# Attention values and output projection by token tile, in matmuls of 512 columns

## The reference, cut to what matters

```python
h = rms_norm(x, norm_mix)
z = h @ w_in                        # queries, keys, values of branch A, gates ga, gb, ...
oa = moba_attention(qa, ka, va, bias_a) @ w_oa
ob = dsa_attention(qb, kb, vb, q_idx, k_idx, w_idx, bias_b) @ w_ob
x = x + (sigmoid(ga) * oa + sigmoid(gb) * ob) @ w_out
x = x + memory_cross_attention(rms_norm(x, norm_x), rms_norm(mem, mem_norm), wq, wk, wv, wo)
x = x + hier_moe(rms_norm(x, norm_moe), ...)   # 32 experts, 2 per token; w1, w3, w2: 6 MB each expert
return rms_norm(x, final_norm)
```

## Time and profile before

| | us |
|---|---|
| median of 3 runs | 676.24 |
| lowest, highest | 675.78, 677.32 |
| the profiled execution | 677.62 |
| its span | 675.8 |
| PE busy in it | 508.3 (75%) |
| DVE, ACT busy | 204.1 (30%), 145.3 (21%) |
| moved by transfers | 244.21 MB, mean 361 GB/s |
| mean granted PE clock | 0.88 |

### The profile page before, as it was taken

The page is one execution under the profiler, slowest core; times in us unless marked ns, Lnnn a source line. Parts: engine busy times, 40 slices in busy tenths (PEclk is TensorE's granted clock), DMA queues, the critical chain, the costliest instruction groups (busy, mean ns, idle before and its releaser), DMA issues.

```text
span 675.8 us, 8749 instructions
## 1 busy us (share of the span) xinstructions
PE 508.3 (75%) x3793; PEld 322.9 (48%) x3793; DVE 204.1 (30%) x376; ACT 145.3 (21%) x252; POOL 16.5 (2%) x31
## 2 busy tenths in 40 slices
PE   7999999999999997966834835773474567347475
PEld 6999998899999752421401411231131123114121
DVE  4799655488857431100000100000010000001002
ACT  5665555354535421000000000000000000000002
POOL 1200010001001000000000000000000000000001
PEclk8999999999999998996867978785798869679779
DMA  9899433607899999999999999999999999999994
GB/s 291 257 324 366 184 125 125 249 1 261 299 392 384 405 387 430 429 426 429 428 428 430 424 432 427 427 430 423 432 428 426 430 427 428 429 426 430 426 407 158
DMA packets 48825, 244.21 MB, mean 361 GB/s; under 512 B 9032, under 2 KB 18704, under 8 KB 37264
## 3 DMA queue, kind: packets, MB, share of 16 engines
q1 hardware_dynamic: 48784, 243.62, 89.3%
HBM read 242.53 MB, written 4.22 MB: 365 GB/s over the span
## 4 chain that ended last, share of the span: by engine, by line
PE 52%; DMA 43%; SPq 2%; issue 1%; ACT 0%; DVE 0%; PEld 0%; POOL 0%; POOLq 0%; PEldq 0%; DVEq 0%
PE ps L707 16%; DMA slots_late<-in_w 13%; PE ps L1065 11%; DMA slots_own<-in_w 9%; DMA attn_data<-in_w 7%; PE ps L730 7%; PE ps L1070 6%; DMA slot_last<-in_w 5%; DMA slot_mixed<-in_w 5%; DMA slot_spare<-in_w 3%; PE ps L685 1%; PE ps L758 1%; SPq L542 1%; PE ps L824 1%; PE ps L853 1%; PE ps L1174 1%
## 5 line engine op out<-in xcount | busy, mean ns | idle before, releaser
L1065 PE MATMUL ps<-slots_late,x_sb 128*32 128x512 f32 x320 | 85.4, 676 | 35.9 <-DMA slots_late<-in_w 14.1
L1065 PE MATMUL ps<-attn_data,x_sb 128*32 128x512 f32 x160 | 63.4, 700 | 12.4 <-DMA slots_own<-in_w 12.4
L1065 PE MATMUL ps<-slot_spare,x_sb 128*32 128x512 f32 x128 | 59.6, 664 | 15.9 <-DMA attn_data<-in_w 15.9
L1801 DVE TENSOR_TENSOR slot_extra<-ps,slot_extra 128x512 f32<-128x512 f32 x8 | 5.5, 692 | 213.0 <-ACT slot_extra L1428 213.0
L433 DVE TENSOR_TENSOR w_low<-slots_own,w_high 128x2048 fp32r<-128x2048 f32 (+1 forms) x32 | 64.6, 2021 | 15.9 <-ACT w_high L1238 15.7
L1425 ACT ACTIVATE slot_extra<-ps 128x256 f32<-128x256 f32 x8 | 3.1, 383 | 299.6 <-PE ps L1132 299.6
L1065 PE MATMUL ps<-slots_own,x_sb 128*32 128x512 f32 x240 | 55.5, 654 | 9.5 <-DMA slot_spare<-in_w 3.9
L1070 PE MATMUL ps<-slots_own,slot_extra 128*32 128x512 f32 x192 | 49.0, 715 | 17.1 <-DMA slots_late<-in_w 8.3
L1238 ACT ACTIVATE w_high<-slots_own 128x2048 fp32r<-128x2048 f32 (+1 forms) x32 | 54.2, 1696 | 18.4 <-PE ps L730 10.8
L1070 PE MATMUL ps<-attn_data,slot_extra 128*32 128x512 f32 x112 | 45.8, 747 | 15.1 <-DMA slots_own<-in_w 15.1
L707 PE MATMUL ps<-h_high,w_high 128*128 128x256 f32 x224 | 55.4, 288 | 0.0
(11 more groups left out here) (258 smaller groups left out, 869.5 us busy)
## 6 DMA issues: line engine op xcount, KB each, us to landing
slots_own<-in_w SPq DMA_DIRECT2D x27, 2048.0 KB, 32.7
slots_late<-in_w SPq DMA_DIRECT2D x25, 2048.0 KB, 35.0
attn_data<-in_w SPq DMA_DIRECT2D x16, 2048.0 KB, 34.2
slot_last<-in_w SPq DMA_DIRECT2D x9, 2048.0 KB, 34.9
slots_own<-in_w_in SPq DMA_DIRECT2D x8, 2048.0 KB, 12.1
slot_spare<-in_w SPq DMA_DIRECT2D x8, 2048.0 KB, 35.4
slot_mixed<-in_w SPq DMA_DIRECT2D x7, 2048.0 KB, 35.0
slots_own<-in_w_out SPq DMA_DIRECT2D x2, 2048.0 KB, 8.5
```

The costliest lines, as they stand in the source:

```text
L1065: return pe.matmul(ps[SLOTS * e:SLOTS * e + SLOTS, 4 + matrix, :], xeT[:, k, SLOTS * e:SLOTS * e + SLOTS], w, start=(k == 0), stop=(k == K ...
```

## The change

Two helpers are added. `half_depths` computes the first or second half of the depths of two jobs at once: of 512 weight columns, for both token tiles, in matmuls of 128 x 512. A job is now one token tile by 512 columns, and a unit of split weights is 4 depths by 512 columns (the same size as before). `keep_warm` issues matmuls of zeros. The rest follows from this: which bank comes free when, what the additions and turns wait for, and in what order ACT and DVE do their part. Beside this, units 8 and 9 of the expert weights come in halves, and one `start_sum` moves.

```diff
-EARLY_HALF = {10: 0, 11: 1}
+EARLY_HALF = {8: 0, 9: 0, 10: 0, 11: 1}
+FIRST_HALVES = ("av0", "out0", "out2")
 # weights()
+            if stem in ("av", "out"):
+                return c, w512(c)[:, 4 * (i % 2):4 * (i % 2) + 4, :]
 # sync, behind the load into place 3
                     weights_split(sp, "vm")
-                    load_half(10, EARLY_HALF[10], early_half_in[10])
+                    for early in (10, 8, 9):
+                        load_half(early, EARLY_HALF[early], early_half_in[early])
 # tensor
 gains_turned():
                 pe.transpose(ps[:, 1, 0:KD], gain_rows, ident[0:KD, 0:KD]).then_inc(gain0_turned, 1)
+                keep_warm(1)
 turn_residual(b):
-                pe.wait_ge(resid_set, b + 1)
+                pe.wait_ge(resid_set, b // 2 * 2 + 2)
+            def half_depths(tiles, second, ready=None):
+                unit = tiles[second]
+                wh, wl = part(w_high, unit), part(w_low, unit)
+                for low in range(2):
+                    if low:
+                        weights_split(pe, unit)
+                    else:
+                        pe.wait_ge(split_high, SPLITS.index(unit) + 1)
+                    for t in range(TT):
+                        if not second and not low:
+                            begin(tiles[t])
+                        o = ps[:, job(tiles[t])[0], :]
+                        for k in range(4):
+                            depth = 4 * second + k
+                            if ready and t + low == 0:
+                                ready(depth)
+                            for x_ in (h[:1] if low else h):
+                                m = pe.matmul(o, x_[:, depth, t * P:(t + 1) * P], (wl if low else wh)[:, k, :],
+                                              start=(depth + low == 0 and x_ is h[0]),
+                                              stop=(low == 1 and depth == KD - 1), skip_group_check=True)
+                        if second and low:
+                            end(m, tiles[t])
+                if not second:
+                    m.then_inc(wide_used, 1)
+            def keep_warm(n):
+                for _ in range(n):
+                    pe.matmul(ps[:, 6, 0:P], score[:, 0:P], score[:, 0:P], start=True, stop=True)
             pe.wait_ge(zeros_set, 1)
-            for _ in range(14):
-                pe.matmul(ps[:, 6, 0:P], score[:, 0:P], score[:, 0:P], start=True, stop=True)
+            keep_warm(16)
             turn(xn, xn_set, gains_turned)
+            keep_warm(2)
-            split_rows("av0", h)
+            half_depths(("av0", "av1"), 0)
             scores(0)
-            split_rows("av1", h)
+            half_depths(("av0", "av1"), 1)
-            for i in range(4):
-                split_rows(f"out{i}", h, merged_ready if i == 0 else None)
-                if i:
-                    turn_residual(i - 1)
+            for i in range(2):
+                half_depths(("out0", "out1"), i, merged_ready)
+            half_depths(("out2", "out3"), 0)
+            turn_residual(0)
+            turn_residual(1)
+            half_depths(("out2", "out3"), 1)
             query_products(0, q0, range(4))
+            turn_residual(2)
             turn_residual(3)
-            start_sum(1, 0)                # of the three ahead of the routing
+                    start_sum(1, 0)        # beside the fourth, in step 0
 # scalar: split_weights(u)
+                if u >= 2 and SPLITS[u - 2] in FIRST_HALVES:
+                    act.wait_ge(wide_used, FIRST_HALVES.index(SPLITS[u - 2]) + 1)
+                elif u >= 2:
 # scalar: values
-            for i in range(2):
-                copy_job(f"av{i}", av[:, :, 256 * i:256 * i + 256], by_rows)
-                after(f"av{i}")
-                if i == 0:
-                    exps(0)
+            after("av0")
+            exps(0)
+            for t in range(TT):
+                copy_job(f"av{t}", av[:, t, :])
+            after("av1")
 # scalar: output projection
+            after("out0")
+            after("out1")
+            split_turned(2, 0, 2, tT_high)
+            split_turned(2, 1, 2, tT_high)
+            after("out2")
+            act.wait_ge(resid_set, 3)
             square(x_sb[:, 0, :], 2, 0, xn[:, 0, :], squares[0])
+            split_turned(2, 2, 2, tT_high)
             split_turned(2, 3, 2, tT_high)
 # vector: output projection
+            after("out0")
+            for t in range(TT):
+                add_residual(f"out{t}", x_sb[:, t, 0:512], resid_set)
+            after("out1")
+            split_turned(2, 0, 2, tT_high, tT_low)
+            split_turned(2, 1, 2, tT_high, tT_low)
+            after("out2")
+            for t in range(TT):
+                add_residual(f"out{2 + t}", x_sb[:, t, 512:1024], resid_set)
+            split_turned(2, 2, 2, tT_high, tT_low)
             square(x_sb[:, 1, :], 2, xn[:, 1, :])
             split_turned(2, 3, 2, tT_high, tT_low)
```

More of the change, by code:

```diff
@@ L124 @@
           + [f"ob{i}" for i in range(4)] + ["km"] + [f"out{i}" for i in range(4)] + ["qx", "vm"])
+assert SPLITS.index("qx") % 2 == EARLY_HALF[8] and SPLITS[-1] == "vm"
+FIRST_HALVES = ("av0", "out0", "out2")
 STEP_JOBS = [("av0", "av1"), ("ga0", "ga1"), ("ga2", "ga3"), ("bq0", "bq1"), (None, "gb0"), ("gb1", "oa0"),
@@ L313, in decoder_layer @@
         h_high_set, h_low_set = sem("h_high_set"), sem("h_low_set")
-        split_high = sem("split_high")
+        split_high, wide_used = sem("split_high"), sem("wide_used")
         low_set = (sem("low_set_v"), sem("low_set_p"))
@@ L1234, in split_weights @@
                 weights_landed(act, name)
-                if u >= 2:
+                if u >= 2 and SPLITS[u - 2] in FIRST_HALVES:
+                    act.wait_ge(wide_used, FIRST_HALVES.index(SPLITS[u - 2]) + 1)
+                elif u >= 2:
                     job_computed(act, SPLITS[u - 2])
```

## The result

The changed kernel takes 679.75 us, median of 20 runs (675.13 to 683.47); the kernel before took 676.26 in the 20 runs beside it (674.58 to 680.16). The ratio is 1.0045 (95% interval 1.0029 to 1.006): slower, clear of noise, by 3.5 us between the medians and 3.0 by the ratio, where 673.7 was forecast. The changed kernel's runs lie 8.3 us apart; those of the kernel before lie 5.6 apart, and 3.0 without the one at 680.16.

A forecast was written before the change was run, and what follows sets the result against it. TensorE's chain was taken to bound the first 250 us, the weight stream the expert part; values 1.2 plus output projection 1.3 gave 2.5 us off the 676.24 median, so 673.7 us, 8-in-10 range 672.3 to 676.5.

The forecast's parts named there:

- The values' term: Attention values on TensorE: wide calls let gate job ga0 start at 68.5, not 69.74; 1.2 us taken, bounds 0 to 1.24.
- at SP's own pace: Bias transfer ahead of ga0: asked for independently of PE, landing at 63.9 whatever PE does.
- Warming: Zero matmuls near the first turns: keep the clock up, PE up to 2.4 us earlier at 21; booked 0.
- this gain ends at the place above: Start of ga0: warming's earlier PE is stopped by the bias, since ga0 can't start before 68.5.
- Rival E: Before the router: PE idles 0.86 us more, clock drops to 1.2 GHz before the first request; 677.6 us, chance 0.08.
- Width: Split projections: one 512-column fp32r matmul costs 0.2145 us against two of 256 at 0.240; a call 5.15 us.
- Output projection: Output projection through queries: four wide calls save 2.4 us, new 1.0 us wait ahead of qx0; 1.3 gain taken.
- Rival C: Wide matmuls bring little or twos cost more: output loses 0.45 to gains 0.5, values 0 to 1.2; 675.6, chance 0.20.
- The halves and the third start_sum: Half transfers of expert units 8 and 9 fill a dip; the moved sum lies where PE waits anyway; 0 booked.
- the request moves the end: First further expert weights, asked for at 246.34: bringing that forward brings the end forward by the same amount.
- Rival D: Weight stream not done when the request comes earlier: only its own 1.2 us comes through; 675.0 us, chance 0.07.
- Rival B: Front gains more: warming's 2 us pass 68.5 because the bias lands earlier too; 671.7 us, chance 0.10.

The follow-up runs named there:

- a_cold: Changed kernel without its added warming (14 zero matmuls at the start, none between or behind the turns): 681.53 us, ratio 1.0084.
- a_kept_warm: Changed kernel with 14 matmuls on the identity between the values and ga0: 678.89 us, ratio 1.0048.
- a_bias_late: Changed kernel with one added 1 MB transfer right ahead of the bias read: 683.97 us, ratio 1.011.
- a_copies_first: Changed kernel with ACT's copies of the values ahead of exps(0) and DVE's low split of ga0 ahead of logits(0): 675.13 us, ratio 0.9981.
- a_narrow_values: Changed kernel with the values in two narrow jobs again, av0 copied ahead of exps(0): 675.82 us, ratio 0.9993.
- b_wide_values: Kernel before with only the values in wide matmuls and both copies behind exps(0): 678.7 us, ratio 1.0036.
- probe: Changed kernel with six forms of matmul, eight each, between the two calls of the values, into an unread bank: 692.34 us, one run, time not compared.
- b_warm: Kernel before with only the added warming (16, 1 and 2 matmuls of zeros): 675.6 us, ratio 0.9993.
- b_again: Kernel before, unchanged, profiled once more: 674.39 us in that execution.
- a_bias_early: Changed kernel with SP asking for the three bias transfers earlier, ahead of other loads: 678.47 us, ratio 1.0032.

## Why the prediction was wrong

**The values' term: gain 1.24, bound 0 below. This step failed.** I wrote that the bias "lands at 63.9 whatever PE does" and let ga0 start at 68.5 from it. The mechanism behind that was right: ga0 starts behind ACT's copy of av0, behind exps(0), 4.50 us after the first scores (64.98 to 69.48, and the same in a_cold, a_kept_warm and a_bias_late), where I had 4.55. What was wrong is that the landing was taken for a constant, and that the wait for it was priced at nothing. In the changed kernel's profile the first scores came at 64.98, 1.03 later, so ga0 gained 0.26 at its start instead of 1.24; and the wait of 3.12 let the clock fall, with which ga0 took 7.52 instead of 5.76 (1.5 of it the clock, the rest the start after a wait). The term came out at a loss of 1.5. That the order of the copies is the cause is shown from both sides: a_copies_first and a_narrow_values take the loss away, b_wide_values makes most of it.

I also wrote that the bias is asked for "at SP's own pace". It is not: SP waits until the copy within DRAM has landed (35.87 + 17.79 in the changed kernel's chain), and asks then. SyncE's rows for the read of the bias in the kernel before, profiled again, in the changed kernel, and in a_copies_first:

```profile
52.74 0.37 SPq L504 DMA_DIRECT2D attn_data<-bias_rep_dram  x1
```
```profile
53.68 0.37 SPq L509 DMA_DIRECT2D attn_data<-bias_rep_dram  x1
```
```profile
55.80 0.37 SPq L509 DMA_DIRECT2D attn_data<-bias_rep_dram  x1
```

In the nine profiled executions that leave the bias path alone (the probe aside), the first scores came at 63.70, 63.95, 64.21, 64.54, 64.98, 65.30, 66.96, 67.05 and 67.73, each after a wait. The copy was asked for at 35.2 to 37.3 and took 16.4 to 18.6 us, the read behind it 11 to 13. The old order takes such landings in its slack (a_narrow_values and b_warm, the two latest of the nine, have it and stand at 0.9993). The new order pays for any landing behind 61.7: its values are done at 66.2.

Not shown is how far the landing moves within one kernel. The nine are of eight kernels; the one profiled twice had 63.95 and 64.21. So that the landing makes the 8.3 us of spread is argued, from a_copies_first, which has 1.4 in ten runs. As an estimate from this record: the clock can give 1.5 of the 8.3 and the part behind the request 2.3, so the landing would have to move by some 4.5, about what the nine show (4.0).

My 1.24 was, besides, the difference to 69.74, a start that the low clock at 12 us had made late. Against b_again's 67.52, ga0 at 69.48 is a loss of 2.0 before the clock's 1.5. I had tested the wait against DVE's row of it, but never asked how far that row can move.

**Warming: booked 0, but it isn't free.** It did make TensorE earlier at the values (54.20 to 57.18), and "this gain ends at the place above" was right as far as it went. But the low clock that it was to cure was that of one execution; b_again had 1.00 without it, and in the old order its earlier TensorE came through. In the new order being early turned into idling: 3.12 us, after which the clock fell and ga0 cost 1.5 more. Rival E had that mechanism, and looked for it at the wrong place. The sum had nothing for it. That the warming is nevertheless not what costs most shows in a_cold and b_wide_values. In profiles without added warming the bias was asked for at 52.3 to 52.8 (four), with it at 53.7 to 55.8 (five); whether an earlier TensorE delays the bias through the loads that it sets off is open.

**Width: the term was mis-sized.** Starts are 0.227 to 0.23 apart (54.20, 54.43), not 0.2145; a call is 5.5 us, not 5.15. The starts lie midway between the value taken and my bound of 0.240, no gain at all. The two calls with their scores save 0.5 us, not 1.4. The Trainium skill (TensorE: Matmul & The Clock Gate, section Back-to-back issue gap) gives 131 ns sustained for 512 columns and, by its formula for one matmul alone, about 216: the trace agrees with neither for this kind, and bears out my rejection of the first. The probe's bfloat16 form, at 0.216, agrees with the second.

**Output projection: 0 instead of 1.3.** From 185.86 the four calls and two turns end at about 208.64, 22.8 us, where the jobs with their turns took 23.9: 1.1 saved of the 2.4 that I had. The new wait ahead of the queries is there, behind DVE's addition, and is smaller than I had it (0.47, not 1.0). From 209.26 to 216.38 the queries take 7.12 us, before 6.19, 0.9 more, and with the longer wait this takes back the rest. That it is because splits and scalings now come in twos is argued, not tested. Rival C's walk, 24 matmuls of 0.240 a call, had this stretch at a loss of 0.45; mine at 1.3 gained; the 0 lies between them.

**What held.** The halves and the third start_sum, booked 0: a_narrow_values equals b_warm, though only together with the output projection. That the request moves the end held within 2.3 us (428.5 to 430.8 behind it in thirteen profiles), not more closely. Rival D, a stream that isn't done when the request comes earlier, wasn't put to the test by the change, whose request came later; in a_copies_first and b_again it came 2.0 and 2.2 earlier, and the part behind it was no longer (429.5 and 428.5). Rival E at the router: 1.00 at 242. Rival B, a front that gains more, had its sign wrong.

## What to carry to other kernels

Before a copy, an evacuation or a split is put behind work that waits for a transfer, take the slack of the old order as a quantity (here 3.4 us) and set it against the spread of that transfer's landing over several executions, not against one trace; and price the wait itself, the fallen clock behind it too. A profile of the kernel before is one draw: a second one would have shown the clock at 12 us at 1.00, ga0 and the request 2.2 earlier, and so a gain at ga0 that wasn't there. It would not have shown the landing, which was the same within 0.26. The repair is cheap where it is only an order: free the bank that the bottleneck waits for first (a_copies_first: 675.13, ten runs within 1.4 us, faster than the changed kernel by 4.6 and than the kernel before by 0.2%).

## What the runs showed of the hardware

A wait of 3.12 us on TensorE took the granted clock to 0.50 in the job behind it (17 products 0.213 instead of 0.120 apart, 1.5 us), and so did one of 6.95; waits of 1.16 to 1.39 us ahead of the same job left it at 1.00 in a_cold, b_wide_values and a_bias_early. Small matmuls in place of the idle time, 28 records in 3.29 us, kept it at 1.00. An fp32r matmul of 512 columns takes 0.227 us where two of 256 take 0.240, half a full-precision record of the same width 0.2145, and a bfloat16 matmul 0.216. The read of the bias, in nine profiled executions of eight kernels, was asked for anywhere from 52.3 to 55.8 us.
